# First rank weights issued by ScalarE's queue, the norm gain turned by TensorE, first products on a cleared tile, and output weights loaded slot by slot

## What is computed

```python
xn = rms_norm(h, pre_norm[i])            # h * rsqrt(mean(h*h) + eps) * pre_norm
proj = xn @ w_in[i]                      # split into 14 column groups
log_a = log_sigmoid(g_a @ gla_a_up[i] + gla_a_bias[i]) / GLA_TAU
o_gla = gla_mixer(g_q, g_k, g_v, log_a)  # gated, group-normed, times silu(g_z)
o_nsa = nsa_mixer(n_q, n_kc, n_vc, ...)  # compressed, selected and window attention
mixed = concat([o_gla, o_nsa]) @ w_out[i]
h = h + rms_norm(mixed, post_norm[i])
gate = sigmoid(h @ ple_gate[i])
h = h + rms_norm((p[i] @ ple_proj[i]) * gate, ple_norm[i])
```

## Time and profile before

| | |
|---|---|
| median of 3 runs | 802.61 us (801.17 to 802.99) |
| profiled execution | 802.57 us, span in the trace 800.8 us |
| TensorE busy | 783.2 us, 98% of the span |
| VectorE, ScalarE, GpSimd busy | 498.0, 421.5, 429.3 us |
| chain that ended last | TensorE 89%, VectorE 6%, ScalarE 3% |
| transfers | 58.38 MB in 39920 packets |

### The profile page before, as it was taken

The page is one execution under the profiler, slowest core; times in us unless marked ns, Lnnn a source line. Parts: engine busy times, 40 slices in busy tenths (PEclk is TensorE's granted clock), DMA queues, the critical chain, the costliest instruction groups (busy, mean ns, idle before and its releaser), DMA issues.

```text
span 800.8 us, 12540 instructions
## 1 busy us (share of the span) xinstructions
PE 783.2 (98%) x4570; PEld 667.7 (83%) x4570; DVE 498.0 (62%) x981; ACT 421.5 (53%) x893; POOL 429.3 (54%) x434
## 2 busy tenths in 40 slices
PE   7999999999999999999999999999999999999995
PEld 7878898888888888888789888999888888888884
DVE  2783359981670504556999999999950273525526
ACT  4601064213331214767999889999952624435434
POOL 3302125527132121577899988989945473653653
PEclk9999999999999999999999999999999999999998
DMA  9511111201111111263200000000077232332347
GB/s 308 124 46 51 40 40 38 66 22 45 41 40 42 38 43 37 79 160 75 66 2 2 1 1 2 1 3 1 2 253 260 79 106 80 99 98 79 93 126 229
DMA packets 39920, 58.38 MB, mean 73 GB/s; under 512 B 11281, under 2 KB 17713, under 8 KB 39858
## 3 DMA queue, kind: packets, MB, share of 16 engines
q1 hardware_dynamic: 39570, 56.52, 23.7%
q0 software_dynamic: 288, 1.05, 0.8%
HBM read 49.16 MB, written 5.25 MB: 68 GB/s over the span
## 4 chain that ended last, share of the span: by engine, by line
PE 89%; DVE 6%; ACT 3%; issue 1%; POOL 1%; DMA 0%; DVEq 0%; SPq 0%; ACTq 0%; POOLq 0%
PE psum L1075 46%; PE psum L1374 7%; PE psum L1352 4%; PE psum L1353 4%; PE psum L1397 4%; PE psum L1398 4%; PE psum L1191 3%; DVE gla_att L2234 2%; DVE gla_b L2225 1%; PE psum L1242 1%; PE psum L997 1%; PE psum L995 1%; PE psum L996 1%; PE psum L1101 1%; PE psum L1330 1%
## 5 line engine op out<-in xcount | busy, mean ns | idle before, releaser
L1875 POOL TENSOR_TENSOR w_lo<-w_raw,w_hi 128x512 fp32r<-128x512 f32 x124 | 178.7, 1446 | 300.5 <-ACT w_hi L1520 299.9
L1520 ACT ACTIVATE w_hi<-w_raw 128x512 fp32r<-128x512 f32 x124 | 78.1, 634 | 301.2 <-PE psum L1075 280.1
L1075 PE MATMUL psum<-w_hi,xT_hi 128*128 128x512 f32 x256 | 100.5, 393 | 0.0
L1075 PE MATMUL psum<-w_hi,xT_lo 128*128 128x512 f32 x256 | 99.7, 389 | 0.0
L1075 PE MATMUL psum<-w_lo,xT_hi 128*128 128x512 f32 x256 | 99.6, 389 | 0.0
L2386 DVE TENSOR_TENSOR pT_lo<-psum,pT_hi 128x512 fp32r<-128x512 f32 (+1 forms) x148 | 93.4, 654 | 1.6 <-ACT pT_hi L1751 0.7
L1751 ACT ACTIVATE pT_hi<-psum 128x512 fp32r<-128x512 f32 (+1 forms) x148 | 82.0, 573 | 7.9 <-PE psum L1374 3.6
L1949 POOL TENSOR_TENSOR p_slc<-p_slc,gate_over_sum 128x512 f32<-128x512 f32 x79 | 80.5, 1043 | 0.9
L1352 PE MATMUL psum<-kT,qT_hi_lo 128*128 128x384 f32 (+3 forms) x192 | 66.3, 350 | 0.9 <-DVE neg_max L2350 0.9
L1353 PE MATMUL psum<-kT,qT_hi_lo 128*128 128x384 f32 (+3 forms) x192 | 60.2, 328 | 0.0
L1397 PE MATMUL psum<-pT_hi,v_hi_lo 128*128 128x512 f32 x132 | 57.7, 437 | 0.0
(11 more groups left out here) (297 smaller groups left out, 1900.2 us busy)
## 6 DMA issues: line engine op xcount, KB each, us to landing
w_raw<-in_w_in SPq DMA_DIRECT2D x56, 256.0 KB, 2.7
w_raw<-in_ple_gate SPq DMA_DIRECT2D x32, 256.0 KB, 2.5
w_raw<-in_w_out SPq DMA_DIRECT2D x30, 256.0 KB, 2.7
x_tok<-in_x SPq DMA_DIRECT2D x8, 512.0 KB, 8.0
h_tok<-in_x SPq DMA_DIRECT2D x8, 512.0 KB, 5.9
kT<-kT SPq DMA_DIRECT2D x12, 256.0 KB, 3.6
out<-h_tok SPq DMA_DIRECT2D x6, 512.0 KB, 5.5
w_raw<-in_ple_proj SPq DMA_DIRECT2D x8, 256.0 KB, 2.5
```

What stands on the lines that cost most here:

```text
L1075: mm = pe.matmul(out, lhs, rhs, start=(first and n == 0), stop=(final and n == 2))
L1520: act.activation(w_hi(i)[:, 0:w], w_in(i)[:, 0:w], ACT.Copy).then_inc(s_whi, 1)
L1875: pool.tensor_tensor(w_lo(i)[:, 0:w], w_in(i)[:, 0:w], w_hi(i)[:, 0:w].bitcast(F32), ALU.subtract).then_inc(s_wlo, 1)
```

## The change

The rank weights' nine transfers move from SyncE's stream to the head of ScalarE's, ahead of its wait for the constants and of its table load. SyncE then issues all eight tiles of x in a row. The gain is fetched as 8 rows of 128 values (`GPR`); TensorE turns them into a PSUM bank, and ScalarE copies them to `gpre`. VectorE clears a tile (`WU`) before any wait, and TensorE multiplies it twice before it waits for the constants; one of the four fillers goes. ScalarE takes `split_hi(u)` before `take_hi(u)` for the first four units. At the end of the attention each of the first three output weights waits for the last unit that uses the buffer under its own slot; the transfer of `p` and those of x for the residual move behind the third weight and a wait for all units.

```diff
@@ -146,6 +146,8 @@
     RT = sb("inv_rms_rows", [P, SEQ], F32, R4 + 4096)
     RTZ = sb("inv_rms_rows_again", [P, SEQ], F32, R4 + 16384)
     DR = sb("inv_rms_diag", [P, 2, 4, P], F32, R5)
+    GPR = sb("pre_gain_rows", [KD, P], F32, R5 + 8192)
+    WU = sb("warm_up", [P, 256], F32, R5 + 12288)
     DUMP = sb("square_dumps", [P, 2, DM], F32, R5 + 8192)
     AGR = sb("rank_w_raw", [P, KD, 304], F32, R7)
     AGW = sb("rank_w_lo48_hi", [P, KD, RROWS + 256], F32R, R3)
@@ -269,6 +271,9 @@
 
     s_const = sem("const_in")
     s_small = sem("small_in")
+    s_wu = sem("warm_up_cleared")
+    s_gptr = sem("pre_gain_turned")
+    s_gpre = sem("pre_gain_read")
     s_x = [sem(f"x_in{i}") for i in range(NT)]
     s_ssq_d = sem("x_sumsq_dve")
     s_rms = sem("x_rms")
@@ -835,18 +840,10 @@
     def _(sp):
 
         sp.dma_start(CT[:], a["consts"]).then_inc(s_const, 16)
-        sp.dma_start(gpre[:], a["pre_norm"][0].rearrange("(k p) -> p k", p=P),
-                     allow_slow_non_contiguous=True).then_inc(s_const, 16)
+        sp.dma_start(GPR[:], a["pre_norm"][0].rearrange("(k p) -> k p", p=P)).then_inc(s_const, 16)
 
         def load_x(t):
             sp.dma_start(XN[:, t], a["x"][0, t * P:(t + 1) * P, :]).then_inc(s_x[t], 16)
-
-        def load_rank_pieces(n):
-            lo, hi = LOADS[n]
-            rows, w = slice(lo * P, hi * P), a["w_in"][0]
-            for at, col, size in ((0, NG_, 32), (32, GA, RANK), (48, NKC, 256)):
-                sp.dma_start(AGR[:, lo:hi, at:at + size],
-                             w[rows, col:col + size].rearrange("(k p) c -> p k c", p=P)).then_inc(s_ag[n], 16)
 
         def load_piece(i):
             c, k = piece[i]
@@ -882,8 +879,6 @@
 
         load_x(0)
         load_x(1)
-        for n in range(len(LOADS)):
-            load_rank_pieces(n)
         for t in range(2, NT):
             load_x(t)
         sp.wait_ge(s_padz, 1)
@@ -930,13 +925,15 @@
                 odd_keys(n % 2, n // 2)
 
 
-        sp.wait_ge(s_pv, len(units))
         for i in range(piece0[cidx["woA"]] + 2, len(piece)):
+            if i < piece0[cidx["woA"]] + 2 + RAW:
+                sp.wait_ge(s_pv, max(u for u in range(len(units)) if u % 4 == i % RAW) + 1)
             load_piece(i)
             n = i - piece0[cidx["woA"]] - RAW
-            if n == 0:
+            if n == 1:
+                sp.wait_ge(s_pv, len(units))
                 sp.dma_start(PR[:], a["p"][0, 0].rearrange("(t p) d -> p t d", p=P)).then_inc(s_pin, 16)
-            elif 0 < n <= NT:
+            if 0 < n <= NT:
                 sp.dma_start(H[:, n - 1], a["x"][0, (n - 1) * P:n * P, :]).then_inc(s_h, 16)
             elif n == NT + 1:
                 sp.dma_start(GPO[:], a["post_norm"][0].partition_broadcast(P)).then_inc(s_gn, 16)
@@ -960,6 +957,9 @@
     @block.tensor
     def _(pe):
 
+        pe.wait_ge(s_wu, 1)
+        for _ in range(2):
+            pe.matmul(bank(0)[:, 0:256], WU[:, 0:P], WU[:], start=True, stop=True)
         pe.wait_ge(s_const, 32)
 
         def turn_x(u):
@@ -1009,7 +1009,8 @@
             for _ in range(n):
                 pe.matmul(bank(0)[:, 0:256], ident, CT[:, 0:256], start=True, stop=True)
 
-        keep_busy(4)
+        pe.transpose(bank(1)[:, 0:KD], GPR[:], ident[0:KD, 0:KD]).then_inc(s_gptr, 1)
+        keep_busy(3)
         for t in range(2):
             pe.wait_ge(s_x[t], 16)
             for u in range(4):
@@ -1506,8 +1507,20 @@
             act.wait_ge(s_a, chain[0])
 
 
+        def load_rank_pieces(n):
+            lo, hi = LOADS[n]
+            rows, w = slice(lo * P, hi * P), a["w_in"][0]
+            for at, col, size in ((0, NG_, 32), (32, GA, RANK), (48, NKC, 256)):
+                act.dma_start(AGR[:, lo:hi, at:at + size],
+                             w[rows, col:col + size].rearrange("(k p) c -> p k c", p=P)).then_inc(s_ag[n], 16)
+
+        for n in range(len(LOADS)):
+            load_rank_pieces(n)
         act.wait_ge(s_const, 32)
         act.activation(first_table[:], CT[:, C_ONE:C_ONE + 2], ACT.Copy)
+        act.wait_ge(s_gptr, 1)
+        act.activation(gpre[:], bank(1)[:, 0:KD], ACT.Copy).then_inc(s_gpre, 1)
+        act.wait_ge(s_gpre, 1)
 
         def split_hi(i):
 
@@ -1532,8 +1545,8 @@
             link(act.activation(DUMP[:, 0], XN[:, t], ACT.Square, accum_out=st[:, 0, t:t + 1]))
 
         for u in range(4):
+            split_hi(u)
             take_hi(u)
-            split_hi(u)
         for u in range(4, KD):
             split_hi(u)
         for u in range(4, KD):
@@ -2022,6 +2035,7 @@
             ins.then_inc(s_d, 1)
             dve.wait_ge(s_d, chain[0])
 
+        dve.memset(WU[:], 0.0).then_inc(s_wu, 1)
         dve.wait_ge(s_const, 32)
 
         def sum_squares(n):
```

## The result

The kernel with the change takes 811.29 us (median of 4 runs, 810.33 to 812.03). The kernel before takes 802.42 beside it (4 runs, 801.17 to 802.99). The ratio is 1.0105, with a 95% interval of 1.009 to 1.0121. The profiled execution took 810.33 us, span 808.5. The forecast was 800.3 and the top of its range 802.6: the sign was wrong.

A forecast was written before the change was run, and what follows sets the result against it. TensorE, busy 783.2 of 800.8 us, was taken as the bound, so an earlier start shortens the total: first rank product 2.0 us earlier plus 0.3 in pace, 802.57 - 2.3 = 800.3 us; 8-in-10 range 799.3 to 802.6.

The forecast's parts named there:

- the part on the transfers: Start, input transfers: small packets fall away, 1.1 us gained; 704 KB of rank weights share the time, 1.9 us.
- The delay that it did price, of x's first two tiles: Start: second tile of x lands between 5.3 and 8.2, needed at about 7.4; at 8.2 it costs 0.5 us.
- ScalarE's nine issues: Head of ScalarE's stream: nine rank-weight issues take 5.00 us as on SyncE, 0.56 each, ending at 5.73.
- ScalarE issues too slowly: Rival, 10 in 100: slower issues delay ScalarE's first read of x; 801.6 at 0.70 each, 803.8 at 0.95 throughout.
- The transfers are the bound: Rival, 15 in 100: mixing queues loses what small packets free, x's last tile still lands at 21.35; time 801.4.
- The clock rises no earlier: Rival, 12 in 100: clock rises at 9.2 as before, fillers and turns run at half speed; gain 1.4, time 801.2.
- The slots: End of attention, output weights by slot: first load 1.4 us earlier, but no product waits for it; costed at nothing.
- first read of turned x: ScalarE at the start: after issues, table, constants, gain and high half, it starts at 8.0 against 9.39.
- first rank product: TensorE at the start: ScalarE's path decides, product starts at 9.8 against 11.79, 2.0 us earlier.
- gain in pace, second to fourth block: Rank products after the first: GpSimd's lead removes its hold on the pace, taken at 0.3 us.
- last tile of x landed: Start, transfers: x's last tile lands at 20.25 instead of 21.35, just in time for turns at 20.3.
- TensorE's path: Start: cleared-tile products, turned gain, fillers and turns leave TensorE free for the first rank product at 9.5.

The follow-up runs named there:

- experiment 1: Changed kernel with the nine rank-weight transfers put back in SyncE's stream, behind the first two tiles of x: 801.09 us, ratio 0.9983 to the kernel before.

## Why the prediction was wrong

**The step that failed** is in the part on the transfers: "In return up to 704 KB of rank weights, 1.9 us at 363 GB/s, share the time." It priced the sharing by bytes, and in one direction: weights delaying x. That x would delay the weights is a term that the sum doesn't have, and so put at nothing without a reason. In the runs the queues share by packets, and a packet was one row of the transfer: the nine need 8 blocks x 128 rows x 3 pieces = 3072 of them, while x's eight tiles are 1024. The page of the changed kernel counts 3216 packets on that queue over the span, these and 144 = 9 x 16 others. So x's last tile landed 4.6 us earlier than before (16.75 against 21.35), and blocks 1 to 3 of the weights 8.5 us later (17.74 against 5.17 + 4.1 = 9.27). No line of the prediction asked when the weights would land. The trace before could have warned: 1195 packets moved 0.32 MB in one window and 198 moved 0.73 MB in the next. I read that as small packets being slow, not as what a queue of them gets beside a queue of large ones. The delay that it did price, of x's first two tiles, came to 1.2 us of waiting for TensorE ahead of the turns (0.98 and 0.20) and decided nothing.

The rule was at hand. The Trainium skill's "DMA: Bandwidth & Descriptors", section Queues, rings and completion order, says that each DMA engine goes round between the queue rows that have work, a packet at a time. The trace agrees with that (424 to 426), and by it the forecast would have been slower. The same section of the Trainium skill gives 9 to 17 descriptors as typical of a packet. Here the profile counts one packet for a row, and by that count the queues alternate (105 to 105 from 10 to 11 us), so the number of rows is what decided. The prediction cites another section of the same page of the Trainium skill, on issuing engines, and took from it that the transfers interleave and that a second issuer saves only issue time, not how they take turns.

**The second step, mis-sized:** ScalarE's nine issues, forecast at 5.00 us, took 10.07. The forecast named issues over 0.7 each as the sign of being wrong, and they were 1.12. The first five were cheaper than forecast (0.46 on average against 0.56). Three of the other four were held longer, up to 4.48 us, with earlier packets of the queue still to pass; with x held back or in short rows, where those passed sooner, the nine took 7.18 and 7.29. SyncE meanwhile went on issuing. That the unpassed packets hold the issue fits all of this but was not tested by itself. So the rival "ScalarE issues too slowly" had the right side, but its cause is the smaller part of the loss. It gave 803.8. With 10.07 in the prediction's own sum, the first read of x would start at 13.0 and the first product at 14.8 (measured 12.79 and 14.66), and the time would be 805.3; the rest, to the profiled 810.33, is the landing of the weights with the low clock behind it. By themselves, with x held back, the issues cost 1.3 us on the version that issues from SyncE (802.41 against 801.09).

**The other rivals.** "The transfers are the bound" feared that mixing two queues loses bytes; none were lost (394 GB/s from 10 to 14 us), only their order was wrong. "The clock rises no earlier" did not happen: the changed kernel turned the first tile of x from 7.05 us at 0.14 a turn or less (eight in 1.09), not at 0.20.

**The steps that held.** The slots cost and gave nothing that shows. The steps of the start, measured with the weights on SyncE:

| step | forecast | measured there |
|---|---|---|
| constants and gain in | 3.4 | 3.09 |
| first read of turned x | 8.0 | 8.14 |
| first rank product | 9.8 | 10.03 |
| gain in pace, second to fourth block | 0.3 | 3.17 - 2.85 (11.03 to 13.88) = 0.3 |
| last tile of x landed | 20.25 | 9.91 + 9.7 = 19.6 |
| turns of the last tiles | 20.3 | 20.61 |

The output products stayed in one piece with the slots, as the chain of the changed kernel shows, beside its row:

```profile
592.51 43.53 PE psum L1076 x192
```

So the forecast described the version that leaves the issue where it was. Its agreement there is partly luck: ScalarE's start was worked out from issues that it doesn't make in that version, and what set its first read there was the landing of the first weights (7.50) and the turns. TensorE's path came later than forecast (9.5): the sixteen turns of x took 2.65 us where one and a half at 0.20 and the rest at 0.11 would be 1.9, and its fillers ended just as the product started. So the two paths end close together there, and which of them decides differs between executions: in the second profile TensorE waits 0.43 us for VectorE's half of x. (The turn of the gain is one pass in the trace, not two; it cost the 0.2 us that it was given.)

## What to carry to other kernels

Before moving transfers to a second queue, count the packets of both queues over the same stretch: the queue with short rows gets as many turns as the other, not as many bytes. Ask of every moved transfer when it lands, not only what it delays; here SyncE's order (two tiles of x, the weights, the rest of x) was doing that work. And an engine that computes should not stand behind more issues than its queue takes without waiting.

## What the runs showed of the hardware

- While both held packets, two queues took turns by packet at every row size tried: with rows of 4 KB, 424 to 426 against rows of 64 and 128 bytes and 45 to 47 against rows of 1 KB (4 to 5 us of the changed kernel); with rows of 2 KB 357 to 365, with rows of 1 KB 1011 to 1005.
- ScalarE's first five issues took 0.41 to 0.51 us each, later ones up to 4.48 us, with the engine's computing instructions behind them, while the queue's earlier packets waited. How much a queue takes before it holds its issuer I didn't measure.
- The time at which TensorE's pitch falls to that of the upper clock differs between executions of one kernel. With the weights on SyncE the same file was profiled twice, and its first six fillers started at 3.38 us both times. They took 2.93 us in the execution shown under experiment 1. In the other:

```profile
3.38 2.27 PE L1019 MATMUL psum<-consts 128*128 128x256 f32 x6
7.10 1.09 PE L1027 MATMUL psum<-consts,x_tok 128*128 128x128 f32 x8 [0.31 <-DMA x_tok<-in_x]
```

Here the pitch fell within the fillers, before 5.7 us; in the other execution only within the turns, which took 2.65 us. The Trainium skill's "TensorE: Matmul & The Clock Gate", Part 1, says that the monitor runs freely against the kernel's start; these rows agree. The earlier rise brought little: the second tile of x was then waited for, 0.31 us.
